# Transposed inputs moved from 32 to 64 bytes past the weight rings (modulo 128)

## The reference

```
first block:
  x = LN(a*x + (B * conv3(C * h)) @ w_out)       [B, C, h] = x @ w_in
  x = LN(a*x + relu(x @ w1)^2 @ w2)              1024 -> 4096 -> 1024
  x = LN(a*x + latent_attention(x))              8 heads, block-causal
  x = LN(a*x + relu(x @ w1)^2 @ w2)
second block:
  x = x + gate0 * (rglru(mod(rms(x))) @ w_out)   gated linear recurrence
  x = x + gate1 * (attention(mod(rms(x))) @ w_out)
  return rms(x) * g
```

## The kernel before, in words

| tiles | before | after |
|---|---|---|
| raw, w_high, w_low, x, z | 0 | 0 |
| xT_h, xT_l | 32 | 64 |
| stage, rows, consts, ones, cols | 64 | 0 |
| modcol, buf_a, buf_b, hT_h, hT_l, kT, area, small, prm | 0 | 0 |

## Time and profile before

### The profile page before, as it was taken

The page is one execution under the profiler, slowest core; times in us unless marked ns, Lnnn a source line. Parts: engine busy times, 40 slices in busy tenths (PEclk is TensorE's granted clock), DMA queues, the critical chain, the costliest instruction groups (busy, mean ns, idle before and its releaser), DMA issues.

```text
span 768.6 us, 12084 instructions
## 1 busy us (share of the span) xinstructions
PE 757.9 (99%) x4982; PEld 689.4 (90%) x4982; DVE 586.4 (76%) x786; ACT 405.1 (53%) x512; POOL 34.6 (5%) x66
## 2 busy tenths in 40 slices
PE   8999999999999999999999999999999999999996
PEld 8999889999999889888889999998799987999985
DVE  4886898978688697787988777677688877666654
ACT  5455235545444424875355444434748968754632
POOL 0000000000000011000000000000500051000001
PEclk9999999999999999999999999999999999999999
DMA  9977538897867631446488978876226354754102
GB/s 343 340 271 275 195 128 320 335 367 280 322 245 297 266 124 63 165 148 263 170 318 336 344 289 304 318 278 244 96 99 224 112 210 168 276 214 165 55 6 79
DMA packets 26983, 173.94 MB, mean 226 GB/s; under 512 B 3248, under 2 KB 3632, under 8 KB 7856
## 3 DMA queue, kind: packets, MB, share of 16 engines
q1 hardware_dynamic: 26640, 173.14, 60.8%
q10 hardware_dynamic: 288, 0.02, 0.0%
HBM read 172.10 MB, written 1.05 MB: 225 GB/s over the span
## 4 chain that ended last, share of the span: by engine, by line
PE 96%; ACT 1%; DMA 1%; DVE 1%; POOL 0%; issue 0%; SPq 0%; POOLq 0%; ACTq 0%
PE bank L581 12%; PE bank L582 12%; PE bank L583 12%; PE Y L716 11%; PE Y L717 11%; PE Y L719 11%; PE bank L1070 2%; PE bank L1071 2%; PE bank L1072 2%; PE bank L999 2%; PE Y L741 1%; PE bank L1036 1%; PE bank L819 1%; PE bank L648 1%; PE bank L1037 1%; PE bank L645 1%
## 5 line engine op out<-in xcount | busy, mean ns | idle before, releaser
L1613 DVE TENSOR_TENSOR w_low<-raw,w_high 128x2048 fp32r<-128x2048 f32 (+3 forms) x125 | 278.9, 2239 | 66.2 <-ACT w_high L1206 63.6
L1206 ACT CAST w_high<-raw 128x2048 fp32r<-128x2048 f32 (+3 forms) x125 | 232.7, 1871 | 94.2 <-DMA raw<-weights 83.1
L581 PE MATMUL bank<-xT_h,w_high 128*128 128x256 f32 x728 | 203.7, 280 | 0.0
L582 PE MATMUL bank<-xT_l,w_high 128*128 128x256 f32 x728 | 203.2, 279 | 0.0
L583 PE MATMUL bank<-xT_h,w_low 128*128 128x256 f32 x728 | 203.1, 279 | 0.0
L581 PEld LDWEIGHTS bank<-xT_h,w_high 128*128 128x128 f32 x728 | 136.8, 188 | 1.3 <-DVE w_low L1613 0.3
L582 PEld LDWEIGHTS bank<-xT_l,w_high 128*128 128x128 f32 x728 | 136.9, 188 | 1.1
L583 PEld LDWEIGHTS bank<-xT_h,w_low 128*128 128x128 f32 x728 | 136.9, 188 | 0.0
L716 PE MATMUL Y<-w_high,hT_h 128*128 128x512 f32 x324 | 126.8, 391 | 0.0
L717 PE MATMUL Y<-w_low,hT_h 128*128 128x512 f32 x324 | 126.5, 390 | 0.0
L719 PE MATMUL Y<-w_high,hT_l 128*128 128x512 f32 x324 | 99.9, 390 | 0.0
(11 more groups left out here) (291 smaller groups left out, 1143.3 us busy)
## 6 DMA issues: line engine op xcount, KB each, us to landing
raw<-weights SPq DMA_DIRECT2D x149, 1024.0 KB, 5.1
rows<-rows_in SPq DMA_DIRECT2D x9, 512.0 KB, 7.7
raw<-weights SPq DMA_DIRECT2D x4, 576.0 KB, 3.7
z<-gates_in SPq DMA_DIRECT2D x4, 512.0 KB, 3.9
raw<-weights SPq DMA_DIRECT2D x2, 896.0 KB, 4.5
raw<-weights SPq DMA_DIRECT2D x3, 512.0 KB, 7.6
x<-x_in SPq DMA_DIRECT2D x2, 512.0 KB, 4.8
kT<-rows_in SPq DMA_DIRECT2D x2, 512.0 KB, 8.7
```

The source lines that it names most:

```text
L581: mm(dst, high, xh[:, kt, :], start=kt == 0, stop=False)
L582: mm(dst, high, xl[:, kt, :], start=False, stop=False)
L1206: nc.scalar.copy(w_high[:, n % RING, start:COLS[n]], raw[:, s % RAW, start:COLS[n]]).then_inc(w_high_ready, 1)
L1613: tt(w_low[:, n % RING, start:COLS[n]], slot[:, start:COLS[n]], f32(w_high[:, n % RING, start:COLS[n]]), ALU.subtract).then_inc(raw_done, 1)
```

## The change

Three sizes of unused tiles change; no instruction does.

```diff
@@ build(): the tiles in SBUF
         x = sb("x", [P, TB, D])
         z = sb("z", [P, TB, D])
-        sb("space_1", [P, 8])
+        sb("space_1", [P, 16])
         xT_h = sb("xT_h", [P, KT, SEQ], F32R)
         xT_l = sb("xT_l", [P, KT, SEQ], F32R)
-        sb("space_2", [P, 8])
+        sb("space_2", [P, 16])
         stage = sb("stage", [P, 2, 512])
         rows = sb("rows", [P, 2, D])
         consts = sb("consts", [P, 2 * P + 2 * SEQ])
         ones = sb("ones", [P, P])
         cols = sb("cols", [P, NCOL])
-        sb("space_0", [P, 8])
+        sb("space_0", [P, 24])
         modcol = sb("modcol", [P, 2 * NMOD])
```

## The result

The changed kernel takes 776.8 us (median of four executions) against 769.8: ratio 1.0086, 95% interval 1.0073 to 1.0100. It is slower, where 766.6 us was forecast, and outside the range. One of its four executions ran at a lower granted clock (0.851) and is left out of the ratio; the median of the other three is 776.5 us.

What follows compares the result with a forecast made beforehand. The prediction took the pace at which TensorE's matmuls follow each other as the bound. Terms of -4.0, +1.0 and -0.1 us summed to -3.1, from 769.7 to 766.6 us; the range over all was 761.7 to 775.5.

Steps and rivals of the forecast that it cites:

- The sign that the prediction had set for a wrong premise: Products on hT: L716 to L719 not still at 226.7 ns, or L1070 not at 120.0, means hT did not stay.
- first rival: Products on xT: only distance modulo 64 counts, so xT at 64 runs as at 0; +5.4 us, 775.1; chance 0.37 (or worse).
- Term 1: 2400 matmuls of 256 columns with xT moving: -1.65 ns each, -4.0 us; bounds -7.9 and +7.5 us.
- Half of the second step: xT moving: from 32 to 64 bytes gains half of the 3.3 ns seen from 0 to 32, -1.65 ns a matmul.
- Term 2: xT as weights: +1.1 us for 342 of 512 columns, +0.2 for 48 of 448, -0.3 for 258 of 256; together +1.0.
- Term 3: fp32 matmuls on rows, consts and stage, which move too: 1 ns a matmul, 0.1 us less over the kernel.
- Modulo 64: The first rival: xT at 64 paces as at 0, 120.0 and 226.7 ns; 775.1 us, chance 0.37 (or worse).
- Any distance but 0 is alike: Products on xT: 32, 64 and 96 give one pace, so Term 1 and Term 2 vanish; 769.6 us, chance 0.21.

Runs made afterwards that it cites:

- the map: Matmul-only kernel, other engines idle, one ring tile and 16 tiles 0 to 480 bytes from it: 113.3 to 120.1 ns (256 columns, moving), 226.7 to 234.4 (512, stationary).
- (64,0): Matmul-only kernel reading the ring at byte offset 64 and the tile at 0, distance 192: 117.75 and 233.3 ns, against 113.4 and 229.0 expected.

## Why the prediction was wrong

**The bound was right.** The time is the sum of the distances between TensorE's starts; nothing else moved, and no wait of TensorE in the changed kernel is longer than 1.0 us.

**The step that failed** is "everything from modcol on stays modulo 128 [...]. hT therefore keeps its 226.7 and 120.0 ns". The arithmetic of the addresses was right and the modulus was not tested: three places in the trace (0, 32 and -32 bytes) can't tell 128 from 256. The two sums of the spaces, 96 and 224, stood on the page, and their difference is half a period. That step counted 1002 matmuls at nothing; they cost 5.1 us of 5.6, since hT at 128 modulo 256 takes some 233 ns where hT at 0 took 226.7. The sign that the prediction had set for a wrong premise came up: L716 ran at 233.3 ns and L1070 with hT mostly at 118 to 119, not 120.0. No rival covered it, so all ranges stood around the wrong centre. The first rival's 775.1 us came near the measured 776.8 by luck: its 120.0 and 226.7 ns on xT did not occur.

**Term 1** (xT moving, -4.0 us) had the wrong sign: +1.9 us. At 64 nearly all stretches ran at 117.8 ns. "Half of the second step" drew a line through two points of something that is not a line: the map goes 120.0, 117.8, 117.8, 120.1, 118.8, 117.2, 113.3, 118.3. The 113.4 ns taken as the bound exists, at 192 and in the short stretch of the changed kernel at 64, but the entries of this kernel seldom led there. The hint was in the earlier trace rows: 117.8 at the same address as 116.7, which I named and did not follow.

**Term 2** (+1.0 us) had the wrong sign too: -0.6 us. The 342 of 512 columns cost the same, 233.3 ns at both places, where +1.1 was forecast; the 48 of 448 gave back 0.1 us, and those of 256 columns (276 in the trace, not 258) 0.5, since some of their stretches ran at 113.4 ns instead of 118.

**Term 3 and the other engines:** nothing in the runs speaks against them. With stage, rows and consts at the new place and hT back at 0, the time can't be told from that of xT alone; a tenth of a us is too small to be seen.

**The rivals.** "Modulo 64" is refuted for the changed kernel (120.0 was to be seen, 117.6 stands there); its paces at distance 0 were right. "Any distance but 0 is alike" came nearest for xT: 32 and 64 both have 117.8 in the map, and in the kernel they differ by which steady pace the entry leads to, 116.7 in most stretches at 32 and 117.8 in most at 64. It was worth 0.26%, just over what was called telling.

## What to carry to other kernels

When fp32r matmuls follow each other without a wait, the distance between starts is the cost, and here it depended by 6% on where the two SBUF operands lie to each other modulo 256 bytes; before moving a tile, ask what moves behind it and modulo what. Map the pace once with a kernel of matmuls only, then look in the real trace whether a stretch runs at the mapped pace: a slower steady pace at the same addresses can be an entry, and one short matmul can change it. Compare more than one execution before you credit a change with a pace. Read start times, since a difference of 4 ns hardly shows in mean durations: L581 had 278 to 281 ns with xT at 32, 64 and 192.

## What the runs showed of the hardware that was not expected

- A period of 256 bytes for fp32r operands of TensorE, with 113.3 to 120.1 ns for 256 columns in steps of 32 bytes, 122.1 ns in steps of 8, and 226.7 to 234.4 ns for 512 columns.
- The best place is not the same for both roles: moving at 192 (113.3), stationary at 0 (226.7; 229.0 at 192).
- More than one steady pace at one distance: 113.3 and 117.8 at 192, 116.7 and 117.8 at 32, 113.6 and 117.8 at 64, 229.0 and 233.3 for 512 columns at 192. A pace once taken held for 288 matmuls; in the feed-forwards it came back block after block. Only at distance 0 was one pace seen, 120.0 and 226.7.
- Float32 matmuls on kT and z kept 216 ns throughout.
- Left open: what in the array or in SBUF repeats after 256 bytes, why 8 bytes off 192 cost 6.7 ns, whether (64,0) is only an unlucky entry, and whether the entry changes between executions of one kernel.
